# Running sum of the forget gate: made once as rows of eight heads, and added to the scores by two matmuls a head in place of four

## The reference

```python
def forgetting_attention(q, k, v, fg_logit):
    log_f = jax.nn.log_sigmoid(fg_logit.astype(jnp.float32))
    cum = jnp.transpose(jnp.cumsum(log_f, axis=1), (0, 2, 1))
    ...
        s = jnp.einsum('bqhd,bkhd->bhqk', qb, kb).astype(jnp.float32) * ATT_SCALE
        s = s + cum[:, :, start:end, None] - cum[:, :, None, :end]
        ...
        s = jnp.where(ki <= qi, s, NEG)
        p = jax.nn.softmax(s, axis=-1).astype(vb.dtype)
```

## Time and profile before

| | before |
|---|---|
| time, median of 3 runs | 1064.3 us (1063.12 to 1064.83) |
| the profiled execution: time | 1064.01 us |
| its span, first to last instruction | 1061.8 us |
| granted TensorE clock, mean | 0.998 |
| PE busy | 1055.3 us (99%), 7460 matmuls |
| PEld busy | 981.5 us (92%) |
| DVE, ACT, POOL busy | 864.7, 685.4, 347.0 us |

### The profile page before, as it was taken

One profiled execution on the slowest core, in us unless ns is written; L12 is line 12 of the kernel. 1 busy time (PEld: TensorE's weight loads), 2 busy tenths in 40 slices (PEclk: granted clock), 3 DMA queues, 4 the chain that ended last, 5 costly groups with the idle time before them and its releaser, 6 DMA issues.

```text
span 1061.8 us, 21068 instructions
## 1 busy us (share of the span) xinstructions
PE 1055.3 (99%) x7460; PEld 981.5 (92%) x7460; DVE 864.7 (81%) x1582; ACT 685.4 (65%) x1257; POOL 347.0 (33%) x368
## 2 busy tenths in 40 slices
PE   8999999999999999999999999999999999999998
PEld 7999999999999999999989899999998998999998
DVE  7777778776799888887776999888895769998886
ACT  6666766766765655576776766555685667565563
POOL 6222222112255333332121564333350015633331
PEclk9999999999999999999999999999999999999999
DMA  8645454456466555535453666555434436665541
GB/s 287 232 153 161 149 180 150 140 172 205 155 219 216 191 186 183 172 102 182 152 181 121 197 207 205 183 187 191 144 106 142 146 119 199 217 198 185 191 158 41
DMA packets 57972, 183.31 MB, mean 173 GB/s; under 512 B 6448, under 2 KB 10032, under 8 KB 57648
## 3 DMA queue, kind: packets, MB, share of 16 engines
q1 hardware_dynamic: 57040, 181.51, 52.7%
q10 hardware_dynamic: 864, 0.92, 0.3%
HBM read 181.35 MB, written 1.05 MB: 172 GB/s over the span
## 4 chain that ended last, share of the span: by engine, by line
PE 99%; DMA 0%; DVE 0%; issue 0%; ACT 0%; SPq 0%; DVEq 0%
PE ps L407 23%; PE ps L409 12%; PE ps L592 10%; PE ps L594 10%; PE ps L593 9%; PE ps L1646 6%; PE ps L1648 6%; PE ps L1647 6%; PE ps L1130 2%; PE ps L1131 2%; PE ps L1132 2%; PE ps L750 1%; PE ps L795 1%; PE ps L723 1%; PE ps L762 1%; PE ps L781 1%
## 5 line engine op out<-in xcount | busy, mean ns | idle before, releaser
L368 DVE TENSOR_TENSOR w_lo<-w_raw,w_hi 128x1024 fp32r<-128x1024 f32 (+2 forms) x371 | 447.1, 1220 | 48.5 <-ACT w_hi L360 48.0
L360 ACT ACTIVATE w_hi<-w_raw 128x1024 fp32r<-128x1024 f32 (+2 forms) x371 | 355.4, 971 | 153.7 <-PE ps L409 128.7
L407 PE MATMUL ps<-xg,w_hi 128*128 128x512 f32 x1056 | 371.6, 396 | 0.0
L409 PE MATMUL ps<-xg,w_lo 128*128 128x256 f32 x1056 | 293.0, 278 | 0.0
L407 PEld LDWEIGHTS ps<-xg,w_hi 128*128 128x128 f32 x1056 | 198.0, 188 | 44.2
L592 PE MATMUL ps<-w_hi,xg 128*128 128x384 f32 (+1 forms) x576 | 200.3, 348 | 2.0 <-DVE w_lo L387 2.0
L409 PEld LDWEIGHTS ps<-xg,w_lo 128*128 128x128 f32 x1056 | 198.4, 188 | 0.2
L594 PE MATMUL ps<-w_hi,xg 128*128 128x384 f32 (+1 forms) x576 | 193.8, 336 | 0.0
L1768 POOL TENSOR_TENSOR prob_t<-prob_t,qkT 128x256 f32<-128x256 f32 x63 | 100.4, 1593 | 285.5 <-ACT prob_t L1691 285.5
L593 PE MATMUL ps<-w_lo,xg 128*128 128x384 f32 (+1 forms) x576 | 193.5, 336 | 0.0
L1646 PE MATMUL ps<-g_hi,w_hi 128*128 128x256 f32 x528 | 147.9, 280 | 0.0
(11 more groups left out here) (174 smaller groups left out, 1372.8 us busy)
## 6 DMA issues: line engine op xcount, KB each, us to landing
w_raw<-w_stream SPq DMA_DIRECT2D x228, 512.0 KB, 3.6
w_raw<-w_stream SPq DMA_DIRECT2D x139, 384.0 KB, 3.4
w_raw<-w_stream SPq DMA_DIRECT2D x4, 392.0 KB, 3.0
xT<-x_a SPq DMA_DIRECT2D x4, 256.0 KB, 6.1
con<-consts SPq DMA_DIRECT2D x1, 1024.0 KB, 8.1
xT<-x_t SPq DMA_DIRECT2D x4, 256.0 KB, 4.9
conv_taps<-taps SPq DMA_DIRECT2D x1, 1024.0 KB, 8.9
par<-params SPq DMA_DIRECT2D x1, 592.0 KB, 6.5
```

The source lines that it names most:

```text
L360: nc.scalar.activation(w_hi[s][:, 0:w], w_raw[s][:, 0:w], ACT.Copy).then_inc(w_hi_done, 1)
L368: nc.vector.tensor_tensor(w_lo[s][:, 0:w], w_raw[s][:, 0:w], w_hi[s][:, 0:w].bitcast(F32), ALU.subtract).then_inc(w_lo_done, 1)
L407: nc.tensor.matmul(bank(b, 0, 2 * TOK), w_hi[s][:, k * P:(k + 1) * P], xg[:, k, :, :].rearrange("p h t -> p (h t)"), start=(k == 0), stop= ...
L409: last = nc.tensor.matmul(bank(b), w_lo[s][:, k * P:(k + 1) * P], xg_hi[:, k, :], start=False, stop=(k == KT - 1), skip_group_check=True)
```

## The change

A new piece, `decay_pe`, makes minus the running sum once for all eight heads, behind chunk 8. Its stationary operand is eight columns of `fg_hi` or `fg_lo`, its moving one `tri`, and its output eight rows of 384 columns in bank 5. It is four matmuls. `decay_act` copies the rows to `decay_hi` (rounded), `decay_dve` makes `decay_lo`. Both tiles have 128 rows, of which GpSimd zeroes all at the start. `score_c_pe` then picks the row of its head: the stationary operand is one column of the identity (`head_row`), broadcast to 128 columns, the moving one `decay_hi` or `decay_lo`, 384 columns. It waits for `decay_lo` (the semaphore `decay` at 3) in place of `fg_lo`. So that the sum is there in time, `fg_hi` moves on ACT from n = 8 to n = 7, ahead of the copy of the queries, and `fg_lo` on DVE ahead of the split of its chunk.

```diff
+    def decay_pe(eng):
+
+        eng.wait_ge(tri_in, 1)
+        eng.wait_ge(fg_lo_done, 1)
+        eng.wait_ge(att[2].ke, 1)
+        for t in range(2):
+            for n, part in enumerate((fg_hi, fg_lo)):
+                last = nc.tensor.matmul(bank(K_BANK, 2 * P * t, 3 * P - 2 * P * t)[0:HEADS_C, :],
+                                        part[:, t * HEADS_C:(t + 1) * HEADS_C], tri[:, 0:3 * P - 2 * P * t],
+                                        start=(t == 0 and n == 0), stop=False, skip_group_check=True)
+        last.then_inc(decay, 1)
+
+    def decay_act(eng):
+        eng.wait_ge(decay, 1)
+        eng.wait_ge(decay_zero, 2)
+        nc.scalar.activation(decay_hi[0:HEADS_C, :], bank(K_BANK, 0, 3 * P)[0:HEADS_C, :], ACT.Copy).then_inc(decay, 1)
+
+    def decay_dve(eng):
+        eng.wait_ge(decay, 2)
+        nc.vector.tensor_tensor(decay_lo[0:HEADS_C, :], bank(K_BANK, 0, 3 * P)[0:HEADS_C, :],
+                                decay_hi[0:HEADS_C, :].bitcast(F32), ALU.subtract).then_inc(decay, 1)
...
-        eng.wait_ge(tri_in, 1)
-        eng.wait_ge(fg_lo_done, 1)
+        eng.wait_ge(decay, 3)
         for h in range(2):
-            for t in range(2):
-                col = t * HEADS_C + 2 * pr + h
-                out = bank(S_BANK + h, 2 * P * t, 3 * P - 2 * P * t)
-                for n, part in enumerate((fg_hi, fg_lo)):
-                    nc.tensor.matmul(out, part[:, col:col + 1].broadcast_to([P, P]), tri[:, 0:3 * P - 2 * P * t],
-                                     start=(t == 0 and n == 0), stop=False, skip_group_check=True)
+            col = 2 * pr + h
+            for n, part in enumerate((decay_hi, decay_lo)):
+                nc.tensor.matmul(bank(S_BANK + h, 0, 3 * P), head_row[:, col:col + 1].broadcast_to([P, P]), part[:],
+                                 start=(n == 0), stop=False, skip_group_check=True)
...
+            if n == 8:
+                decay_pe(eng)
...
+            if n == 7:
+                forget_hi_act(eng)
             if n == 8:
-                forget_hi_act(eng)
+                decay_act(eng)
...
+            if n == 8:
+                forget_lo_dve(eng)
             split_lo(eng, C_QKV + n + AHEAD)
...
             if n == 8:
-                forget_lo_dve(eng)
+                decay_dve(eng)
...
+                nc.scalar.activation(head_row[:], con[:, CON_ID:CON_ID + HEADS_C], ACT.Copy)
...
+            nc.gpsimd.memset(decay_hi[:].bitcast(F32), 0.0).then_inc(decay_zero, 1)
+            nc.gpsimd.memset(decay_lo[:].bitcast(F32), 0.0).then_inc(decay_zero, 1)
```

More of the change, by code:

```diff
@@ L210, in build @@
     fg_lo = sb("fg_lo", [P, 2 * HEADS_C], F32R)
+    head_row = sb("head_row", [P, HEADS_C], F32R)
+    decay_hi = sb("decay_hi", [P, 3 * P], F32R)
+    decay_lo = sb("decay_lo", [P, 3 * P], F32R)
     up_s = [[qkT[b][0][:, s * TOK:(s + 1) * TOK] for s in range(2)] for b in range(2)]
@@ L335, in build @@
     fg_lo_done = sem("fg_lo_done")
+    decay = sem("decay")
+    decay_zero = sem("decay_zero")
     ln_pe = sem("ln_pe")
```

## The result

The changed kernel takes 1065.77 us (median of 17 runs, 1065.28 to 1067.01), the kernel before in the same comparisons 1063.81. The ratio is 1.0019, 95% interval 1.0012 to 1.0025: about 2 us slower, and clear of no change. The forecast was 1063.6, between 1062.4 and 1065.0; the time lies 0.8 us above the range, and the kernel moved the other way than forecast. The 0.88 stood for a change of less than 0.2%, which the prediction took for the limit of what can be told from none. The change is 0.19%, just inside that band, but 17 runs tell it from none. The profiled execution took 1065.88 us, 1.87 more than that of before.

A forecast was written before the change was run, and what follows sets the result against it. The prediction took TensorE as the bound. It summed -1.54 us removed and +0.81 for `decay_pe` to -0.73, giving 1063.3 us from the profiled 1064.01, or 1063.6 for a median, range 1062.4 to 1065.0.

The forecast's parts named there:

- The 0.88: Whole kernel: the chance given to a time within about 0.2%, or 2.1 us, of the kernel before.
- What bounds the kernel: Chain of waits: TensorE 99%, other engines 0%, so work taken from TensorE's queue is worth what it occupies there.
- What is removed, -1.54: Scores blocks: four short matmuls a pair go, saving 0.385 us a pair, 1.54 us over four pairs.
- `decay_pe`, +0.81: Behind chunk 8 on TensorE: four new narrow matmuls cost 0.81 us, with a change of the array's part priced in.
- lower end: `decay_pe` on TensorE if the change of part costs nothing: 0.52 us, or 0.58 with the late follower.
- the change of part is free: Rival, at `decay_pe`: eight fp32r columns pay no change of part; -1.0 us in all, 1063.3 us, chance 0.19.
- The three waits: `decay_pe`, ACT at `decay_hi`, DVE at `decay_lo`: nothing is late; 0.55 us spare at the first, 0.5 at the last.
- The forecast is then -0.73 us: Whole kernel: the sum on TensorE, -1.54 + 0.81, taken from the profiled execution's 1064.01 us.
- the slower one: Rival: scores of pair 0 wait for `decay`; measurably slower from 3.3 us late, 1066.4 us and more, chance 0.05.
- The range: Median of the whole kernel: 1062.4 to 1065.0 us, with scatter, to hold eight in ten.

The follow-up runs named there:

- narrow_fp32: `after_end` with the four matmuls of `decay_pe` in fp32 in place of fp32r; 1064.10 us in one run.
- pad32: The kernel before with one unused tile of 32 bytes a partition ahead of g; 1066.87 us against 1063.87, ratio 1.0030.
- after_end: The changed kernel with `head_row` allocated last, so that g is at 64 modulo 128 bytes as before; 1062.25 us against 1063.64, ratio 0.9987.
- pad64: The kernel before with one unused tile of 64 bytes a partition ahead of g, which then starts at 0 modulo 128; 1069.58 us, ratio 1.0057.
- pad96: The kernel before with 96 unused bytes ahead of g, which then starts at 32 modulo 128; 1066.27 us in one run, MLP stage 186.22.
- xg64: The kernel before with 64 unused bytes ahead of `xg` and 64 behind `fg_lo`, weights and g keeping their places modulo 128; 1063.01 us, ratio 0.9997.
- glo96: The kernel before with `g_lo` alone moved from 64 to 96 modulo 128 bytes; 1067.27 us, MLP stage 186.91.
- ghi96: The kernel before with `g_hi` alone moved to 96 modulo 128 bytes, `g_lo` staying at 64; 1063.66 us, MLP stage 185.81.
- before_x96: The kernel before with `xg` and the mix tiles at 96 modulo 128 bytes, g at 64, nothing of the change; 1060.05 us against 1063.90, ratio 0.9962.
- pad3072: The kernel before with one unused tile of 3072 bytes a partition ahead of g; 1063.66 us, ratio 0.9998.
- front32: The kernel before with an unused tile of 32 bytes ahead of all its tiles, so that all move together; 1063.78 us, ratio 1.0003.

## Why the prediction was wrong, by its own steps

- **What bounds the kernel:** right. From it I concluded that work taken from TensorE is worth what it occupies; what I left out is that the rest of TensorE's work must keep its pace for that.
- **What is removed, -1.54:** right, -1.60.
- **`decay_pe`, +0.81:** mis-sized, 0.52. That is the figure of its lower end, in part by luck: that end had the second short matmul followed after 0.11 us and no late follower, the trace has 0.06 and a follower 0.05 late. The step "I take 0.81, since both neighbouring changes of part ... show the longer distance" took fp32 neighbours for an fp32r instruction. `narrow_fp32` shows that the type decides. And the 0.28 behind the convolution was misread as the price of a change of part: fp32 transposes on 128*128 are followed by 0.26. The rival "the change of part is free" had the right size for this term.
- **The three waits:** right, with 0.5 us to spare at the last.
- **"The forecast is then -0.73 us":** this is the step that failed. The sum had no term for the 22 turns of the three MLP stages, which the change doesn't touch but whose operands it moved by 3104 bytes. They cost +3.43. `pad32` shows this without the change (1.0030), `after_end` shows the change without it (0.9987).
- **The rivals:** the slower one had the wrong mechanism, a late wait; nobody waited. I had looked at the new tiles only for their memsets, and the diff's three `sb(...)` lines ahead of `g_hi` were in front of me.
- **The range** held only costs on the path of the change, and its upper end was 0.8 us short. It also stood on the median of three runs, 1064.3; over 17 runs that of the kernel before is 1063.81, so that the step to the measured time is 2.0 us, not 1.5.

That moving g against the tiles ahead of it, weights and `xg` among them, changes the MLP stages' time is shown, by pads alone. That the reads of the moving operand and of the next weights get in each other's way in SBUF, for which the swing of the distances speaks, is only argued; no run separates it. Nor is there a rule for the pace: `pad64`, `pad96` and `xg64` change the pace of matmuls whose own operands stay, and `glo96` and `ghi96` don't add up. Whether `xg` or a tile behind it makes the gain of `before_x96` is open, and whether 96 is the best place was not searched.

## What to carry to other kernels

When TensorE is full, a new tile is not free even if it is unused: look where it pushes the tiles allocated behind it (here 32 of the 3104 bytes made the whole loss), and allocate new tiles last, or compare with a pad alone. If a change loses where it has changed nothing, follow the start of each matmul along both traces until the difference grows; busy time and waits don't show a loss of 2 ns a matmul. And take the price of an instruction from one of its own type, and the price of a condition from two rows that differ in it alone: fp32 rows did not price fp32r, and the late follower was there without a change of part.

## What the runs showed of the hardware

- 256-column fp32r matmuls, with a new stationary operand each, stand 113.5 to 120 ns apart, by where the operands lie: a down projection of 24 takes 2.72 (`xg64`), 2.83 (before) or 2.88 us (`pad32`).
- With g, `xg` and the weights at the same place modulo 128 bytes, a stage is slowest of the four distances tried: 187.73 against 185.62 us at 64. A shift by 3072 bytes costs nothing (`pad3072`), and neither does one of all tiles together (`front32`).
- Matmuls change their pace when only the operands of their neighbours in the stream have moved. Moving g slowed the up projection from 5.56 to 5.65 us a turn (`pad64`), and moving `xg` and the tiles behind it sped the down projection up, from 2.83 to 2.72 (`xg64`).
- A matmul with eight stationary columns costs no longer step in as fp32r (0.17 us), and does as fp32 (0.26). An fp32 matmul on 128*128 has 0.17 as well, but the second fp32r matmul behind it starts 0.26 after the first in place of 0.17, with or without a change of part.
